# Two-layer hybrid decoder on one core: another order for VectorE's work in a pair of seven products

## The chip, the cores and the metric

The kernel runs on one core of one Trainium2 chip, as one program. The metric is the device time of an execution in microseconds (us), the median of three runs. The engines of the core are PE (TensorE), DVE (VectorE), ACT (ScalarE), POOL (GpSimd) and SP (SyncE, which here only issues DMAs); each runs its own list of instructions in order, and they hand over through semaphores.

## The reference

Two layers over T = 528 tokens (16 learned meta tokens ahead of 512), width 1024, in float32:

```
h = rms_norm(x, norm_g); z = h @ w_in                      # split into 11 parts
y_rnn = (rg_lru(x_rnn, ...) * silu(g_rnn)) @ rg_out
y_sc  = (sc_b * conv(sc_c * x_sc) * silu(g_sc)) @ sc_out
y_att = (mla(c_q, c_kv, k_rope, ...) * silu(g_att)) @ mla_out
gates = sigmoid(gate_logits + gate_b).reshape(b, t, 3, D)
merged = gates[:,:,0] * y_rnn + gates[:,:,1] * y_sc + gates[:,:,2] * y_att
return x + merged @ w_out
```

The change lies in the part that computes `gate_logits = h @ w_gates` for the three gates, and merges.

## The kernel before

**Numbers in two parts.** Every float32 operand of a matmul is held as a high part (rounded, `_hi`) and a low part (the rest, `_lo`), and a product is three matmuls: hi*hi, hi*lo, lo*hi. Weights come from HBM in units of 512 KB (128 partitions x 1024), into two staging buffers `w_raw`, and are split into a ring of four `w_hi` and `w_lo` buffers.

**The stages.** A layer runs NORM, CQ, ATT (four turns), RG (four turns), MR (four turns), MS (four turns), OUT. Only MR and MS are touched. There PE computes, in turn, a pair of gate tiles and one (MR) or two (MS) dense products `y`: MR turn i is pair a, y0, pair g, y1; MS turn i is pair g, y0, y1. The 12 pairs of a layer are PAIR_LIST; the first three (PLAIN) are plain products, the other nine, q = 0 to 8, are done by `seven`: the 2 x 2 block product in seven instead of eight block products (q = 0 to 4 in MR, q = 5 to 8 in MS).

**A pair of seven, engine by engine.** Its two units C and D give the four blocks of weights.
- DVE, `weight_sums(q)` (L1789): waits for both units and makes four sums S1 to S4 in `w_sum`, four instructions.
- ACT, `lead_upper(q, n)` (L1258): the high parts of blocks 0 to 3. Blocks 0 and 1 come from C, 2 from D, 3 is the first sum.
- POOL, `lead(q)` (L550): their low parts, two instructions each. Block 3 also waits for all four sums. Its first instruction raises `unit_split` by 2.
- ACT `sum_upper(q, n)` (L1264) and DVE `sum_lower(q, n)` (L1347): high and low parts of blocks 4 to 6, from the sums, when PE has left the ring's blocks.
- PE, `seven` (L883): products n = 0 to 6, 12 matmuls each. n = 0 waits for slot 0 to be free, n = 2 for slot 1; n = 0 to 3 for `lead_lo`, n = 4 to 6 for `sum_lo`; n = 5 also for gate sum 1, n = 6 for gate sum 2.
- ACT `keep_part` (L1276) and DVE `gate_sums` (L1804 to L1815): the first product is put aside and the block products are added up from PSUM in seven instructions: G1 (L1804) lets n = 5 write its bank, G2 (L1806) lets n = 6 write its own, then G3 (L1808); the last four (L1810, L1812, L1814, L1815) wait for n = 6, and L1814 and L1815 free the slots 0 and 1 for the next pair.
- ACT `open_gates(q)` (L1289): two tanh; the first waits for L1812, the second for both slots to be freed. Behind them DVE's `att_gate` or `merge` uses the gates.

**The order on ACT** (`open_pair`, unchanged): sum_upper(q, 0), keep_part(q), sum_upper(q, 1), sum_upper(q, 2), lead_upper(q+1, 0), lead_upper(q+1, 1), open_gates(q), lead_upper(q+1, 2), lead_upper(q+1, 3).

**The order on POOL**: lead(q), [branch_lower (L569) behind the a pairs], the split of the y unit or units (L471 one instruction, L476 four), lead(q+1).

**The loads on SP** (L383), in order of use: a unit is loaded when the unit two before it is split. So block 3 of lead(q) lets the unit Y of the next y product and unit C of pair q+1 go, and the split of Y lets unit D of pair q+1 go. In MS there are Y0 and Y1: lead(q) lets both go, Y0's split lets C go and Y1's split D.

Of the kernel before, what the change touches and what calls it, by code (L numbers as in the profile page):

```python
# [24 lines left out]
ALU = mybir.AluOpType  # L25
# [58 lines left out]
PLAIN = 3  # L84
# [81 lines left out]
def build(nc, xt, w_units, w_pair, params, hparams, consts, rope, stream):  # L166
    with ExitStack() as ctx:
# [5 lines left out]
        def sem(name):  # L173
            if name not in sems:
                sems[name] = ctx.enter_context(nc.semaphore(name))
            return sems[name]

        def at(name, l, i, k):

            stage, per = SIGNALS[name]  # L180
            first, this = (per, per) if isinstance(per, int) else (per[0], per[l])
            return sem(name), l * (STAGES[stage][0] * first) + i * this + (k + AHEAD.get(name, 0))
# [24 lines left out]
        def freed(stage, tile):  # L207

            return sem(f"slot_free{slot_of(stage, tile)}")
# [147 lines left out]
        def pair_used(l, p):  # L357

            if p < 0:
                return sem("unit_used"), unit_value("RG", l, 3, 5) + (RING + 1)  # L360
            stage, i, name, j = PAIR_LIST[p]
            return sem("unit_used"), unit_value(stage, l, i, j + 1) + (RING + 1)
# [982 lines left out]
        def _(dve):  # L1345
# [40 lines left out]
            for l in range(DEPTH):  # L1386
# [334 lines left out]
                def att_gate(i):  # L1721

                    for n in range(2):
                        dve.wait_ge(*was_read("RG", l, 3, "my1"))
                        dve.wait_ge(*gate_there(2 * i, n))
                        dve.scalar_tensor_tensor(kept(l, tile(xm, i * 2 + n)), kept(l, g_t[n][:]), 1.0,
                                                 kept(l, tile(xm, i * 2 + n)), ALU.add, ALU.mult).then_inc(
                                                     sem("att_gated"), 1)
# [62 lines left out]
                def sum_lower(q, n):  # L1791

                    dve.wait_ge(*at("sum_hi", l, q, n + 1))
                    lo_part(block_of(w_lo, 4 + n), raw_blocks(q)[4 + n], block_of(w_hi, 4 + n), "sum_lo")

                def gate_sums(q):

                    stage, i, name, j = PAIR_LIST[q + PLAIN]
                    w = SIDES[l]
                    bank = lambda s, a: ps[:, s, a, 0:w]  # L1800
                    first, second = (lambda n: g_t[n][:, side(l, 0)]), (lambda n: g_t[n][:, side(l, 1)])
                    dve.wait_ge(*at("block_used", l, q, 2))
                    dve.wait_ge(*at("part_kept", l, q, 1))
                    dve.tensor_tensor(first(0), bank(0, 1), second(0), ALU.add).then_inc(sem("gate_sum"), 1)  # L1804
                    dve.wait_ge(*at("block_used", l, q, 5))
                    dve.tensor_tensor(second(0), bank(0, 0), second(0), ALU.add).then_inc(sem("gate_sum"), 1)  # L1806
                    dve.wait_ge(*at("gate_sum", l, q, 2))
                    dve.tensor_tensor(second(1), bank(1, 0), second(0), ALU.add).then_inc(sem("gate_sum"), 1)  # L1808
                    dve.wait_ge(*pair_used(l, q + PLAIN))
                    dve.tensor_tensor(first(1), bank(0, 0), second(0), ALU.add).then_inc(sem("gate_sum"), 1)  # L1810
                    dve.wait_ge(*at("gate_sum", l, q, 4))
                    dve.tensor_tensor(second(0), bank(0, 1), second(1), ALU.add).then_inc(sem("gate_sum"), 1)  # L1812
                    dve.wait_ge(*at("gate_sum", l, q, 5))
                    dve.tensor_tensor(second(1), bank(0, 0), second(1), ALU.add).then_inc(freed(stage, f"{name}0"), 1)  # L1814
                    dve.tensor_tensor(first(1), bank(1, 1), first(1), ALU.add).then_inc(freed(stage, f"{name}1"), 1)  # L1815

# [84 lines left out]
                weight_sums(0)  # L1903
                mixes_lower(3)
                att_gate(1)
                for p in range(PLAIN, 8):
                    i = p // 2
                    if p % 2 == 0:
                        merge("MR", i - 1, 1)
                    for n in range(3):  # L1910
                        sum_lower(p - PLAIN, n)
                    gate_sums(p - PLAIN)
                    weight_sums(p - PLAIN + 1)
                    if p % 2 == 0:
                        att_gate(i)
                    else:
                        merge("MR", i, 0)
                merge("MR", 3, 1)
                for i in range(4):
                    q = 8 - PLAIN + i  # L1920
                    sum_lower(q, 0)
                    if i:
                        merged_lower(i - 1, 1)
                    sum_lower(q, 1)
                    sum_lower(q, 2)
                    gate_sums(q)
                    if i < 3:
                        weight_sums(q + 1)
                    merge("MS", i, 0)
                    merged_lower(i, 0)  # L1930
                    merge("MS", i, 1)
# [102 lines left out]
```

## Time and profile before

| what | value |
|---|---|
| median of 3 runs | 1707.01 us (1706.09 to 1707.89) |
| the profiled execution: time, span | 1710.13 us, 1708.3 us |
| busy in the span: PE, weight loads, POOL, DVE, ACT | 98%, 92%, 72%, 66%, 34% |
| mean granted TensorE clock | 0.997 |
| the chain that ended last, by engine | PE 74%, DVE 9%, POOL 6%, issue 6%, DMA 4%, ACT 1% |
| pairs of seven, layer 0 and layer 1 | 645.6 to 811.9 us and 1482.6 to 1648.9 us |

The span runs from the first to the last instruction; the 1.8 us around it belong to the run's time. Busy shares are averages over stages with different limits. "Idle before" is the time that an engine stood still ahead of an instruction, with what released it; "issue" means that the view names no releaser.

### The profile page before, as it was taken

How to read it: one execution, taken by the hardware profiler on the slowest of the kernel's cores; microseconds unless marked ns; L12 is line 12 of the kernel's file. 1: busy time of each engine (PE TensorE's matmuls, PEld its weight loads, DVE VectorE, ACT ScalarE, POOL GpSimd, SP SyncE). 2: the span in 40 equal slices, each digit the busy share in tenths (PEclk: the TensorE clock that was granted, in tenths of full speed). 3: DMA queues.
4: the chain of work that ended last, by engine and by line, in shares of the span. 5: the costliest groups of instructions: out<-in, count | busy, mean ns of one | idle time of the engine just before them, and what ended most of it. 6: DMA issues, size and time to landing. Idle time of an engine off the chain costs nothing.

```text
span 1708.3 us, 32114 instructions
## 1 busy us (share of the span) xinstructions
PE 1673.6 (98%) x11840; PEld 1569.9 (92%) x11840; DVE 1120.7 (66%) x1563; ACT 580.6 (34%) x1037; POOL 1228.4 (72%) x1345
## 2 busy tenths in 40 slices
PE   7999999999999999999999999999999999998999
PEld 7999999999999999999998888888889888887887
DVE  6966758485666687666349657574846667877651
ACT  4423333332343423323235232333323434243320
POOL 7764848385888687777867757484868996877684
PEclk9999999999999999999999999999999999999999
DMA  4432322132223232322532323132322223222333
GB/s 161 128 109 62 92 64 88 66 92 80 94 87 95 77 100 87 113 98 94 185 112 88 98 62 109 57 96 71 91 89 87 87 97 100 87 99 99 99 115 134
DMA packets 50008, 164.50 MB, mean 96 GB/s; under 512 B 6112, under 2 KB 7520, under 8 KB 49632
## 3 DMA queue, kind: packets, MB, share of 16 engines
q1 hardware_dynamic: 41904, 146.56, 27.0%
q10 hardware_dynamic: 8032, 17.00, 2.9%
q8 instruction: 44, 0.72, 0.2%
q14 instruction: 28, 0.23, 0.0%
HBM read 152.21 MB, written 10.81 MB: 95 GB/s over the span
## 4 chain that ended last, share of the span: by engine, by line
PE 74%; DVE 9%; POOL 6%; issue 6%; DMA 4%; ACT 1%; ACTq 0%; DVEq 0%; POOLq 0%; SPq 0%
PE slots L610 61%; DMA w_raw<-w_units 4%; PE slots L675 3%; POOL w_lo L476 3%; PE slots L709 3%; PE slots L883 2%; DVE weight_sums L1789 2%; PE slots L771 2%; POOL w_lo L550 2%; PE slots L693 1%; POOL w_hi L471 1%; DVE early L1515 1%; POOL branch_lo L569 1%; DVE early L1530 1%; PE slots L644 1%
## 5 line engine op out<-in xcount | busy, mean ns | idle before, releaser
L476 POOL TENSOR_TENSOR w_lo<-w_raw,w_hi 128x256 fp32r<-128x256 f32 x860 | 741.5, 892 | 17.9
L471 POOL TENSOR_SCALAR w_hi<-w_raw 128x1024 fp32r<-128x1024 f32 x215 | 259.0, 1205 | 245.2 <-PE slots L610 203.4
L610 PE MATMUL slots<-h_hi,w_hi 128*128 128x264 f32 (+1 forms) x1680 | 405.3, 308 | 0.7 <-DVE sc_pad L1643 0.7
L610 PE MATMUL slots<-h_lo,w_hi 128*128 128x264 f32 (+1 forms) x1680 | 399.9, 305 | 0.0
L610 PE MATMUL slots<-h_hi,w_lo 128*128 128x264 f32 (+1 forms) x1680 | 399.4, 304 | 0.0
L610 PEld LDWEIGHTS slots<-h_hi,w_hi 128*128 128x128 f32 x1680 | 271.0, 188 | 14.8 <-issue 1.6
L610 PEld LDWEIGHTS slots<-h_hi,w_lo 128*128 128x128 f32 x1680 | 270.0, 188 | 12.9
L610 PEld LDWEIGHTS slots<-h_lo,w_hi 128*128 128x128 f32 x1680 | 270.3, 188 | 12.0
L610 PE MATMUL slots<-branch_hi,w_hi 128*128 128x264 f32 (+1 forms) x552 | 143.9, 320 | 10.6 <-DVE branch_lo L1360 8.6
L610 PE MATMUL slots<-branch_lo,w_hi 128*128 128x264 f32 (+1 forms) x552 | 142.8, 318 | 0.0
L610 PE MATMUL slots<-branch_hi,w_lo 128*128 128x264 f32 (+1 forms) x552 | 142.4, 317 | 0.0
L550 POOL TENSOR_TENSOR w_lo<-w_raw,w_hi 128x256 fp32r<-128x256 f32 x108 | 89.8, 860 | 39.3 <-ACT w_hi L1258 39.3
L610 PEld LDWEIGHTS slots<-branch_hi,w_hi 128*128 128x128 f32 x552 | 92.2, 191 | 17.7 <-issue 11.1
L610 PEld LDWEIGHTS slots<-branch_hi,w_lo 128*128 128x128 f32 x552 | 91.9, 191 | 6.5
L610 PEld LDWEIGHTS slots<-branch_lo,w_hi 128*128 128x128 f32 x552 | 91.8, 191 | 6.2
L1105 ACT ACTIVATE residual_or_merged<-slots,r_bias,q_sc 128x144 f32<-128x144 f32 (+6 forms) x72 | 44.9, 623 | 149.2 <-DVE r_bias L1592 149.2
L883 PE MATMUL slots<-h_mixes_hi,w_hi 128*128 128x264 f32 (+1 forms) x288 | 82.8, 288 | 8.3 <-DVE w_lo L1347 7.3
L883 PE MATMUL slots<-h_mixes_lo,w_hi 128*128 128x264 f32 (+1 forms) x288 | 81.9, 284 | 0.0
L883 PE MATMUL slots<-h_mixes_hi,w_lo 128*128 128x264 f32 (+1 forms) x288 | 81.9, 284 | 0.0
L1258 ACT ACTIVATE w_hi<-w_raw 128x512 fp32r<-128x512 f32 x54 | 32.7, 628 | 112.7 <-DMA w_raw<-w_units 82.2
L883 PE MATMUL slots<-h_hi,w_hi 128*128 128x264 f32 (+1 forms) x216 | 62.0, 287 | 8.5 <-DVE gate_tanh L1804 8.2
L1347 DVE TENSOR_TENSOR w_lo<-weight_sums,w_hi 128x512 fp32r<-128x512 f32 x54 | 61.6, 1172 | 9.8 <-ACT w_hi L1264 9.8
(276 smaller groups left out, 3681.3 us busy)
## 6 DMA issues: line engine op xcount, KB each, us to landing
w_raw<-w_units SPq DMA_DIRECT2D x251, 512.0 KB, 3.6
stream<-sc_acc ACTq DMA_DIRECT2D x16, 264.0 KB, 2.1
x_old<-stream SPq DMA_DIRECT2D x16, 264.0 KB, 4.1
stream<-residual_or_merged ACTq DMA_DIRECT2D x16, 264.0 KB, 2.6
ab_raw<-w_units SPq DMA_DIRECT2D x8, 512.0 KB, 4.1
residual_or_merged<-xt ACTq DMA_DIRECT2D x4, 528.0 KB, 7.5
stream<-xt ACTq DMA_DIRECT2D x1, 2112.0 KB, 9.7
sc_back<-stream SPq DMA_DIRECT2D x2, 1056.0 KB, 5.8
```

The lines of the kernel that those rows point to most:

```text
L471: pool.tensor_scalar(hi, raw, 1.0, 1.0, ALU.mult, ALU.mult).then_inc(sem("hi_part"), 1)
L476: op = pool.tensor_tensor(lo[:, cols], raw[:, cols], hi[:, cols].bitcast(F32), ALU.subtract)
L550: op = pool.tensor_tensor(lo[:, cols], raw[:, cols], hi[:, cols].bitcast(F32), ALU.subtract)
L610: mm = pe.matmul(out[:, a_, 0:t1 - t0], w(k), x(k)[:, t0:t1], start=(n == 0), stop=(n == 3 * ks - 1))
L675: mm = pe.matmul(bank[:, 0:k1 - k0], q[:, q0:q0 + nq], k[:, k0:k1], start=(m == 0), stop=(m == 4 and not masked))
L709: mm = pe.matmul(out[:, a_, q0 - b0:q1 - b0], v[0:nk, j, h * VHEAD:(h + 1) * VHEAD], pt[0:nk, col + q0:col + q1], start=(j == 0 and n == 0 ...
L771: mm = pe.matmul(out[0:nt_, t % 4 // 2, (t % 2) * 256:(t % 2) * 256 + 256], x[:, k, t0:t0 + nt_], w[0][:, cols], start=(k == 0 and n == 0) ...
L883: mm = pe.matmul(out, block_of(ring, n)[:, k * P:(k + 1) * P], view(x, k), start=(m == 0), stop=(m == 11))
L1105: act.activation(dst, src, ACT.Exp, bias=r_bias[0:nq, n:n + 1], scale=q_sc[0:nq, c:c + 1], accum_out=r_sum[0:nq, n:n + 1]).then_inc(sem("p ...
L1258: act.activation(block_of(w_hi, n), raw_blocks(q)[n], ACT.Copy).then_inc(sem("lead_hi"), 1)
L1347: dve.tensor_tensor(dst, full, hi.bitcast(F32), ALU.subtract).then_inc(sem(signal), 1)
L1789: dve.tensor_tensor(out, x, y, ALU.add).then_inc(sem("w_summed"), 1)
```

## The change

DVE's list within a pair of seven is put in another order; no instruction is added or removed, and no other engine's list changes. Before, a pair is: three lower parts, all seven gate sums, the next pair's weight sums, then gates or merges. After, `gate_sums` comes in three parts and a new function `pair_sums` has the order: lower part 0, (in MS the lower part of the merged tile before), lower part 1, G1, lower part 2, G2 and G3, the next pair's four weight sums, the last four gate sums, then gates or merges.

```
--- before.py
+++ after.py
@@ -1793,26 +1793,29 @@
                     dve.wait_ge(*at("sum_hi", l, q, n + 1))
                     lo_part(block_of(w_lo, 4 + n), raw_blocks(q)[4 + n], block_of(w_hi, 4 + n), "sum_lo")
 
-                def gate_sums(q):
+                def gate_sums(q, part):
 
                     stage, i, name, j = PAIR_LIST[q + PLAIN]
                     w = SIDES[l]
                     bank = lambda s, a: ps[:, s, a, 0:w]
                     first, second = (lambda n: g_t[n][:, side(l, 0)]), (lambda n: g_t[n][:, side(l, 1)])
-                    dve.wait_ge(*at("block_used", l, q, 2))
-                    dve.wait_ge(*at("part_kept", l, q, 1))
-                    dve.tensor_tensor(first(0), bank(0, 1), second(0), ALU.add).then_inc(sem("gate_sum"), 1)
-                    dve.wait_ge(*at("block_used", l, q, 5))
-                    dve.tensor_tensor(second(0), bank(0, 0), second(0), ALU.add).then_inc(sem("gate_sum"), 1)
-                    dve.wait_ge(*at("gate_sum", l, q, 2))
-                    dve.tensor_tensor(second(1), bank(1, 0), second(0), ALU.add).then_inc(sem("gate_sum"), 1)
-                    dve.wait_ge(*pair_used(l, q + PLAIN))
-                    dve.tensor_tensor(first(1), bank(0, 0), second(0), ALU.add).then_inc(sem("gate_sum"), 1)
-                    dve.wait_ge(*at("gate_sum", l, q, 4))
-                    dve.tensor_tensor(second(0), bank(0, 1), second(1), ALU.add).then_inc(sem("gate_sum"), 1)
-                    dve.wait_ge(*at("gate_sum", l, q, 5))
-                    dve.tensor_tensor(second(1), bank(0, 0), second(1), ALU.add).then_inc(freed(stage, f"{name}0"), 1)
-                    dve.tensor_tensor(first(1), bank(1, 1), first(1), ALU.add).then_inc(freed(stage, f"{name}1"), 1)
+                    if part == 0:
+                        dve.wait_ge(*at("block_used", l, q, 2))
+                        dve.wait_ge(*at("part_kept", l, q, 1))
+                        dve.tensor_tensor(first(0), bank(0, 1), second(0), ALU.add).then_inc(sem("gate_sum"), 1)
+                    elif part == 1:
+                        dve.wait_ge(*at("block_used", l, q, 5))
+                        dve.tensor_tensor(second(0), bank(0, 0), second(0), ALU.add).then_inc(sem("gate_sum"), 1)
+                        dve.wait_ge(*at("gate_sum", l, q, 2))
+                        dve.tensor_tensor(second(1), bank(1, 0), second(0), ALU.add).then_inc(sem("gate_sum"), 1)
+                    else:
+                        dve.wait_ge(*pair_used(l, q + PLAIN))
+                        dve.tensor_tensor(first(1), bank(0, 0), second(0), ALU.add).then_inc(sem("gate_sum"), 1)
+                        dve.wait_ge(*at("gate_sum", l, q, 4))
+                        dve.tensor_tensor(second(0), bank(0, 1), second(1), ALU.add).then_inc(sem("gate_sum"), 1)
+                        dve.wait_ge(*at("gate_sum", l, q, 5))
+                        dve.tensor_tensor(second(1), bank(0, 0), second(1), ALU.add).then_inc(freed(stage, f"{name}0"), 1)
+                        dve.tensor_tensor(first(1), bank(1, 1), first(1), ALU.add).then_inc(freed(stage, f"{name}1"), 1)
 
 
 
@@ -1903,29 +1906,31 @@
                 weight_sums(0)
                 mixes_lower(3)
                 att_gate(1)
+                def pair_sums(q, between=None):
+
+                    sum_lower(q, 0)
+                    if between is not None:
+                        merged_lower(between, 1)
+                    sum_lower(q, 1)
+                    gate_sums(q, 0)
+                    sum_lower(q, 2)
+                    gate_sums(q, 1)
+                    if q + PLAIN + 1 < len(PAIR_LIST):
+                        weight_sums(q + 1)
+                    gate_sums(q, 2)
+
                 for p in range(PLAIN, 8):
                     i = p // 2
                     if p % 2 == 0:
                         merge("MR", i - 1, 1)
-                    for n in range(3):
-                        sum_lower(p - PLAIN, n)
-                    gate_sums(p - PLAIN)
-                    weight_sums(p - PLAIN + 1)
+                    pair_sums(p - PLAIN)
                     if p % 2 == 0:
                         att_gate(i)
                     else:
                         merge("MR", i, 0)
                 merge("MR", 3, 1)
                 for i in range(4):
-                    q = 8 - PLAIN + i
-                    sum_lower(q, 0)
-                    if i:
-                        merged_lower(i - 1, 1)
-                    sum_lower(q, 1)
-                    sum_lower(q, 2)
-                    gate_sums(q)
-                    if i < 3:
-                        weight_sums(q + 1)
+                    pair_sums(8 - PLAIN + i, i - 1 if i else None)
                     merge("MS", i, 0)
                     merged_lower(i, 0)
                     merge("MS", i, 1)
```

## Rows read from the trace of the kernel before

**Rows 1.** Who waited for whom: total us, times, longest us

```profile
PE slots L883 <- DVE gate_tanh L1804: 8.2, 6, 1.8
PE slots L883 <- DVE w_lo L1347: 7.3, 6, 1.8
...
DVE weight_sums L1789 <- issue: 39.5, 16, 5.6
```

**Rows 2.** Chain that ended last, in layer 1's pairs: start us, us, what

```profile
1509.17 3.58 POOL w_lo L476 x4
1512.76 3.26 DMA w_raw<-w_units
1518.88 1.24 DVE weight_sums L1789
```

**Rows 3.** Timeline of DVE, layer 0: start us, us, instruction, idle before

```profile
656.03 0.43 DVE L1810 TENSOR_TENSOR gate_tanh<-slots,gate_tanh 128x264 f32<-128x264 f32 x1 [2.00 <-PE slots L883]
...
657.31 0.42 DVE L1815 TENSOR_TENSOR gate_tanh<-slots,gate_tanh 128x264 f32<-128x264 f32 x1
660.06 0.69 DVE L1789 TENSOR_TENSOR weight_sums<-w_raw 128x512 f32<-128x512 f32 x1 [2.32 <-issue]
...
663.07 0.68 DVE L1789 TENSOR_TENSOR weight_sums<-w_raw 128x512 f32<-128x512 f32 x1
...
677.56 0.69 DVE L1789 TENSOR_TENSOR weight_sums<-w_raw 128x512 f32<-128x512 f32 x1 [0.19 <-issue]
...
794.71 0.69 DVE L1789 TENSOR_TENSOR weight_sums<-w_raw 128x512 f32<-128x512 f32 x1 [2.84 <-issue]
```

**Rows 4.** Timeline of ACT, layer 0, around the same pair

```profile
656.96 1.60 ACT L1289 ACTIVATE gate_tanh<-gate_tanh,channel_params 128x528 f32<-128x528 f32 x2 [0.98 <-DVE gate_tanh L1812]
660.00 0.63 ACT L1258 ACTIVATE w_hi<-w_raw 128x512 fp32r<-128x512 f32 x1 [1.43 <-DMA w_raw<-w_units]
```

**Rows 5.** Timeline of POOL, layer 0, around the same pair

```profile
653.54 2.81 POOL L476 TENSOR_TENSOR w_lo<-w_raw,w_hi 128x256 fp32r<-128x256 f32 x4
...
660.71 1.88 POOL L550 TENSOR_TENSOR w_lo<-w_raw,w_hi 128x256 fp32r<-128x256 f32 x2 [1.58 <-ACT w_hi L1258]
663.91 1.90 POOL L550 TENSOR_TENSOR w_lo<-weight_sums,w_hi 128x256 fp32r<-128x256 f32 x2 [1.32 <-DVE weight_sums L1789]
665.78 3.06 POOL L569 TENSOR_TENSOR branch_lo<-sc_back,branch_hi 128x528 fp32r<-128x528 f32 x2
668.81 1.49 POOL L471 TENSOR_SCALAR w_hi<-w_raw 128x1024 fp32r<-128x1024 f32 x1
670.38 3.56 POOL L476 TENSOR_TENSOR w_lo<-w_raw,w_hi 128x256 fp32r<-128x256 f32 x4
```

**Rows 6.** Timeline of SP's DMA issues, layer 0

```profile
673.98 0.33 SPq L383 DMA_DIRECT2D w_raw<-w_units  x1
```

**Rows 7.** Chain that ended last, in layer 0's pairs

```profile
739.43 6.33 PE slots L883 x36
...
757.53 10.24 PE slots L883 x84
767.77 11.72 PE slots L610 x96
```

**Rows 8.** Timeline of DVE, layer 1

```profile
1498.89 0.69 DVE L1789 TENSOR_TENSOR weight_sums<-w_raw 128x512 f32<-128x512 f32 x1 [3.15 <-issue]
...
1633.74 0.69 DVE L1789 TENSOR_TENSOR weight_sums<-w_raw 128x512 f32<-128x512 f32 x1 [4.33 <-issue]
```

**Rows 9.** Timeline of PE: one product 4, and product 2 of each layer's last pair

```profile
739.43 0.51 PE L883 MATMUL slots<-h_mixes_hi,w_hi 128*128 128x264 f32 x1 [1.84 <-DVE w_lo L1347]
...
804.59 0.28 PE L883 MATMUL slots<-h_mixes_hi,w_hi 128*128 128x264 f32 x1
...
1641.50 0.28 PE L883 MATMUL slots<-h_mixes_hi,w_hi 128*128 128x256 f32 x1
```

**Rows 10.** Stretch: PE, weight-load, DVE, ACT, POOL busy (count), PEclk, DMA share, GB/s

```profile
740.00:745.00 5.00, 5.00 (x30) 4.77 (x30) 3.09 (x5) 0.00 (x0) 4.83 (x7) 0.71 0.02 3
```

## The prediction

> **What bounds the kernel now.** I read the page first: PE is busy for 98% of the span, so in the stages without pairs there is nothing to gain, and the change touches none of them. Then the list of waits for PE in the pairs of seven: it stood still for 8.2 us in all ahead of product 5, waiting for G1 (L1804), and for 7.3 us ahead of product 4, waiting for lower part 0 [rows 1]. That is what the new order could win. The same list has the other side: ahead of the weight sums DVE waited 16 times, once in each pair that follows another, 39.5 us in all [rows 1]. "issue" names no releaser, but ACT's lead of block 2 starts at 660.00, released by the DMA of `w_raw` [rows 4], and the weight sums at 660.06 [rows 3]: both wait for unit D. The timelines of DVE, POOL, ACT and SP then give the order of events, and they show a loop beside PE's work. The chain that ended last runs through it in layer 1: split of Y (POOL), DMA of D, weight sums (DVE), and on to POOL again [rows 2].
>
> **The loop, measured.** Call T the start of the weight sums, which is D's landing. For the pair at T = 660.06:
> - the four sums end at 663.75, and POOL starts block 3 at 663.91, T + 3.85 [rows 3, 5];
> - block 3 takes 1.90, branch_lower follows to 668.81 and Y's split to 673.94, that is 1.49 + 3.56 less their overlap, so 10.0 after block 3 began [rows 5];
> - D's DMA is issued at 673.98 and the next weight sums start at 677.56, 3.6 later [rows 3, 6].
> Together 3.85 + 10.0 + 3.6 = 17.5, and 677.56 - 660.06 = 17.50. So this loop, not PE, dates each D. It has seven turns in a layer, from the pair q = 1 to q = 8: 660.06 to 794.71 is 134.65 us in layer 0 [rows 3], and 1498.89 to 1633.74 is 134.85 in layer 1 [rows 8]. PE's own pace is 10.24 for a seven and 11.72 for two y products [rows 7], so 16.1 in MR and 22.0 in MS: near the loop's pace, with no reserve in MR.
>
> **The change part by part.**
>
> *Lower part 2 behind G1, G2 behind it.* G1 moves up by one lower part, so product 5 no longer waits. G2 still ends when it did, since DVE has done the same work by then; PE would win some 1.1 of each 1.3 us. That is worth at most the 8.2 us [rows 1], and only while PE is what ends last.
>
> *The weight sums ahead of the last four gate sums.* Before, L1810 starts at 656.03 and the weight sums at 660.06, after 2.32 of waiting for D [rows 3]. Now DVE sits at the weight sums until 660.06 with the four gate sums behind them. They have the same instructions and durations, so the cost is who waits for them:
> - L1810 begins at T + 3.65. L1812 ends 0.9 later, which is the distance from 656.03 to ACT's tanh at 656.96 [rows 3, 4]; so ACT's tanh starts at T + 4.6. The two take 1.60 [rows 4], to T + 6.2.
> - Behind them in ACT's list stand the high parts of blocks 2 and 3. Before, block 2 went off at 660.00, when D landed [rows 4]; now it starts at T + 6.1 and takes 0.6.
> - POOL starts block 2 at T + 6.75, takes 1.88 and starts block 3 at T + 8.65 [rows 5], against T + 3.85.
> - L1815 ends 1.70 after L1810's start [rows 3], so slot 0 is free at T + 5.2.
>
> *What the loop does with it.* Block 3's first instruction lets Y and C be loaded. The loop gets 8.65 - 3.85 = 4.8 us longer, and nothing takes it up: the DMA of Y, its split and the DMA of D follow in series. Seven turns make 33.6 us a layer. The first turn's T does not move, for nothing ahead of it changes.
>
> *What shortens it again.* In the turns with branch_lower and in MS, Y's split runs beside DVE's lower parts: its four instructions took 3.56 there and 2.81 where DVE was quiet, and the L471 ahead of them was long as well [rows 5]. Together with L471 (1.49 against some 1.1) that is up to 1.2 a turn. In the new order the gates open from T + 5.4, the merges (663.7 to 667.6 before, four instructions of 3.9 in all) end at about T + 9.6 and the lower parts at T + 12. Y lands 0.95 (half of block 3) and 3.6 (a DMA) behind the start of block 3, at T + 13.2, so its split runs beside G1 to G3 only. Five of the seven turns can win this, 6.0 us; the other two are already quiet. Bounds: 27.6 and 33.6 us a layer. I take 28.6, near the quiet row, because DVE is mostly quiet then. The Trainium skill (GPSIMD Engine Reference, Specifications) says that GpSimd's way into SBUF is shared with VectorE and contended by Vector instructions with two SBUF inputs; the rows agree, and by it alone the sum would use 27.6.
>
> *What PE does with it.* In MR the y product now begins at about T + 17.6, when Y is split, and ends at T + 23.5; the next T is 8.65 + 10.0 + 3.6 - 1.0 = T + 21.3, and its slot 0 is free 5.2 later, at T + 26.5. So PE idles 3 us ahead of product 0, 0.7 ahead of product 2 and 1 ahead of Y. In MS a turn of 25 to 26 stands against 22.0. What counts is the last pair of each layer. Its product 2 began at 804.59, T + 9.9, in layer 0 [rows 3, 9] and at 1641.50, T + 7.8, in layer 1 [rows 8, 9]; now it begins at T + 8.75, when block 2 is there, and product 3 another 0.45 late, as block 3 takes 1.9 and a product 1.46 (10.24 / 7 [rows 7]). That is -0.7 in layer 0 and +1.4 in layer 1, less 0.3 of a wait for G1 there that goes. Nothing moves in the tail behind it.
>
> *The sum.* 2 x 28.6 - 0.7 + 1.1 = 57.6 us on the profiled execution's 1710.13 us (span 1708.3 and 1.8 around it). That execution lay 3.1 above the median; on the median it makes 1764.6, and I say 1765. The 8.2 us of waits for G1 are not taken off: PE waits for weights then.
>
> *The clock.* Ahead of one product 4 PE stood still for 1.84 us [rows 9]; in the stretch behind it the granted clock was 0.71, part of it at 1.2 instead of 2.4 GHz [rows 10], and 36 matmuls took 6.33 us [rows 7] where 36/84 of 10.24 is 4.39. The new idle times are as long or longer. One such loss of 1.9 a pair lies in the 3 us of waiting for the slot and costs nothing; in the last pair it shows. Bounds 0 and 4 us for both layers; I take 0 and keep 4 in the range.
>
> **The rivals.**
>
> *Faster: D is there in time.* If D landed before product 6 is near its end, the weight sums would fill the 2.00 us in which DVE waits for PE ahead of L1810 [rows 3], and PE would keep some 7 of the 8.2 us: 1700. It decides where D lands when DVE falls idle, at 654.0 instead of 660.06, some 6 us sooner: then the last gate sums come 3.7 - 2.0 = 1.7 late, and the slots are needed only one y product later. All 16 waits of [rows 1] speak against it: D came last in every pair.
>
> *No change: the loads don't hang on the sums.* If Y and C had been let go early by something else, T would stay, and PE would lose only what shows in the last pairs: -0.7 + 1.1 = 0.4, so 1707.4. The exact sum of 17.50 from the rows speaks against it.
>
> *Much slower: the clock stays down.* If the idle times put whole pairs at 1.2 GHz, a pair of MR would need 32 us of PE, from T + 5.2 to T + 37.4, against the T + 26.5 at which the next may begin: 10.9 more in each of four MR pairs, 44 us a layer, 1853 in all, more with MS. For it: the stretch of [rows 10]. Against it: the same rows, where it passed within the pair. The Trainium skill (TensorE: Matmul & The Clock Gate, section HAM oscillation) says that waits for data between groups of matmuls can put each group back at half rate; for short spells that is the 0 to 4 us above, for whole pairs this rival.
>
> **How the numbers follow.** The lengthened loop has 0.88: it needs only the lists' order and D's landing. D in time 0.05, no change 0.03, the low clock 0.04. The forecast's own range is 2 x 27.6 + 0.4 = 55.6, so 1762.6, to 2 x 33.6 + 0.4 + 4 = 71.6, so 1778.6. I widen it to 1752 to 1781: 10 us below for a loop that gains more from a quiet DVE than those rows show (0.75 us a turn), 2 above for other contention. Within 0.2%, or 3.4 us, a measurement of this kernel can't tell two kernels apart; faster 0.05, same 0.03, slower 0.92.
>
> **What the profile after would show.** Right: block 3 (L550) of each pair starts 8.65 us behind the weight sums; the weight sums from q = 1 to q = 8 lie some 163 us apart instead of 134.65; ACT's block 2 comes behind both tanh; PE waits ahead of product 0 for L1814 (2 to 3 us in MR), ahead of product 2 for L550; the waits for L1804 are gone; PE's busy time is as before or, with the clock, a little longer. Wrong: weight sums that start without a wait; a distance from block 3 to the next T that shrinks by more than 1.2 us; PE busy for much longer at a low granted clock.

## The result and the profile after

The changed kernel took 1748.30 us (median of 4 runs, 1745.45 to 1750.73) against 1707.01 (4 runs, 1706.09 to 1707.89). The ratio is 1.0241, with an interval of 1.0224 to 1.0259: slower by 41 us. The prediction was 1765 us, in a range from 1752 to 1781: its sign came true, and so did the chain of waits that it named; its size was some 17 us too large, which puts the measured time below the range. The profiled execution took 1748.56 us, with a span of 1746.8, which is 38.5 more than before; this is what the account below is held against.

The page of the changed kernel: busy time and share of each engine, and the chain that ended last by engine.

```profile
PE 1685.0 (96%) x11840; PEld 1571.5 (90%) x11840; DVE 1089.2 (62%) x1563; ACT 575.8 (33%) x1037; POOL 1210.2 (69%) x1345
...
PE 68%; DVE 11%; POOL 9%; DMA 6%; issue 4%; ACT 2%; ACTq 0%; DVEq 0%; SPq 0%; POOLq 0%
```

PE has fallen from 74% of the chain to 68%. DVE and POOL stand for more of the chain than before, although both were busy for less of the time (DVE had 66% of the shorter span, POOL 72%). A chain that leaves the busiest engine for engines that are less busy points to a loop of dependencies; the chain itself is shown below.

The waits of the changed kernel: who waited for whom, total us, times, longest us.

```profile
DVE weight_sums L1789 <- DMA w_raw<-w_units: 136.0, 18, 11.5
ACT gate_tanh L1289 <- DVE gate_tanh L1815: 135.0, 18, 10.1
POOL w_lo L550 <- ACT w_hi L1258: 119.7, 24, 8.1
...
PE slots L883 <- DVE gate_tanh L1817: 21.9, 13, 3.0
PE slots L610 <- POOL w_lo L476: 12.8, 13, 1.4
...
PE slots L883 <- POOL w_lo L550: 6.0, 15, 0.7
```

The waits for G1 and for lower part 0 of [rows 1] are gone, as the new order could promise. In their place the first three lines show three engines standing in a row behind one DMA: DVE waits for unit D (136.0 us against 39.5 before), ACT's tanh waits for the gate sums behind DVE's weight sums, and POOL waits for ACT. PE's new waits are for the slot (L1817 frees slot 0), for the split of Y (L476) and for the lower parts of the leads (L550).

The pair that [rows 3 to 5] show before, now after. DVE:

```profile
658.95 0.69 DVE L1789 TENSOR_TENSOR weight_sums<-w_raw 128x512 f32<-128x512 f32 x1 [5.82 <-DMA w_raw<-w_units]
659.68 1.42 DVE L1789 TENSOR_TENSOR weight_sums<-weight_sums,w_raw 128x512 f32<-128x512 f32 x2
661.01 0.69 DVE L1789 TENSOR_TENSOR weight_sums<-w_raw 128x512 f32<-128x512 f32 x1
661.62 0.43 DVE L1813 TENSOR_TENSOR gate_tanh<-slots,gate_tanh 128x264 f32<-128x264 f32 x1
...
679.43 0.69 DVE L1789 TENSOR_TENSOR weight_sums<-w_raw 128x512 f32<-128x512 f32 x1 [6.77 <-DMA w_raw<-w_units]
...
813.64 0.69 DVE L1789 TENSOR_TENSOR weight_sums<-w_raw 128x512 f32<-128x512 f32 x1 [10.46 <-DMA w_raw<-w_units]
```

ACT:

```profile
662.54 1.61 ACT L1289 ACTIVATE gate_tanh<-gate_tanh,channel_params 128x528 f32<-128x528 f32 x2 [7.53 <-DVE gate_tanh L1815]
664.05 0.61 ACT L1258 ACTIVATE w_hi<-w_raw 128x512 fp32r<-128x512 f32 x1
```

POOL:

```profile
664.75 1.44 POOL L550 TENSOR_TENSOR w_lo<-w_raw,w_hi 128x256 fp32r<-128x256 f32 x2 [6.60 <-ACT w_hi L1258]
666.14 2.35 POOL L550 TENSOR_TENSOR w_lo<-weight_sums,w_hi 128x256 fp32r<-128x256 f32 x2
668.45 3.51 POOL L569 TENSOR_TENSOR branch_lo<-sc_back,branch_hi 128x528 fp32r<-128x528 f32 x2
671.92 1.05 POOL L471 TENSOR_SCALAR w_hi<-w_raw 128x1024 fp32r<-128x1024 f32 x1
673.06 2.80 POOL L476 TENSOR_TENSOR w_lo<-w_raw,w_hi 128x256 fp32r<-128x256 f32 x4
```

Read against T = 658.95: L1813 starts at T + 2.67, the tanh at T + 3.6, ACT's block 2 at T + 5.1, POOL's block 2 at T + 5.8 and its block 3 at T + 7.2. The prediction had T + 3.65, 4.6, 6.1, 6.75 and 8.65. So every step is there, in the order forecast, and early by 1.0 from the very first. (Of the fourteen turns in both layers, twelve have block 3 at T + 7.1 to 7.3, and two, q = 1 and q = 5 of layer 1, at T + 7.7.) The reason stands in DVE's rows: the four weight sums took 2.75 us, where they took 3.7 before (660.06 to 663.75 in [rows 3]). POOL's row gives the other 0.4: its two instructions of block 2 took 1.44 and not 1.88.

The chain that ended last, in the same pair: start us, us, what.

```profile
655.39 3.48 DMA w_raw<-w_units
...
658.95 0.70 DVE weight_sums L1789
...
664.05 1.14 ACT w_hi L1258 x2
...
668.49 2.57 POOL branch_lo L569 x2
...
671.92 1.06 POOL w_hi L471
...
673.06 2.81 POOL w_lo L476 x4
675.89 3.46 DMA w_raw<-w_units
```

It is the loop of the prediction, round once, without a single piece of PE. One turn is now 679.43 - 658.95 = 20.48 us, where it was 17.50.

**The account of the 38.5 us.** T is the start of a pair's weight sums, and it moved as follows.

| | layer 0 | layer 1 | forecast, each |
|---|---|---|---|
| first T of the loop (q = 1) to the last (q = 8), before | 134.65 | 134.85 | |
| the same, after (658.95 to 813.64; 1516.80 to 1670.90) | 154.69 | 154.10 | |
| difference | +20.0 | +19.3 | +28.6 |
| of it, T to block 3, seven turns | +23.4 | +24.2 | +33.6 |
| of it, block 3 to the next T, seven turns | -3.4 | -4.9 | -5.0 |
| last T to the y product behind the last pair (811.90 and 830.12; 1648.94 and 1687.28) | -0.7 | +1.2 | -0.7, +1.1 |

Together 20.0 + 19.3 - 0.7 + 1.2 = 39.8; the first T came 1.1 sooner in layer 0, and 0.3 sooner in layer 1 by its distance from that y product of layer 0; 39.8 - 1.4 = 38.4. The line of T to block 3 is off by some 10 us a layer, and it is the one that holds the duration of the weight sums. The last line agrees by luck, as shown further down.

### The profile page after: what moved, and what is told of

Its sections match the earlier page's. It is cut to its first block, busy times and chain, and to the rows that moved or that the text cites. A ratio compares the mean times of both kernels' runs of the same rounds, so it can differ in the third digit from the quotient of the medians.

```text
span 1746.8 us, 32114 instructions
## 1 busy us (share of the span) xinstructions
PE 1685.0 (96%) x11840; PEld 1571.5 (90%) x11840; DVE 1089.2 (62%) x1563; ACT 575.8 (33%) x1037; POOL 1210.2 (69%) x1345
## 4 chain that ended last, share of the span: by engine, by line
PE 68%; DVE 11%; POOL 9%; DMA 6%; issue 4%; ACT 2%; ACTq 0%; DVEq 0%; SPq 0%; POOLq 0%
PE slots L610 58%; DMA w_raw<-w_units 6%; POOL w_lo L476 4%; POOL w_lo L550 3%; PE slots L675 3%; DVE weight_sums L1789 2%; PE slots L709 2%; PE slots L771 2%; POOL w_hi L471 2%; PE slots L693 1%; ACT w_hi L1258 1%; DVE early L1515 1%; POOL branch_lo L569 1%; DVE early L1530 1%; PE slots L644 1%
## 5 line engine op out<-in xcount | busy, mean ns | idle before, releaser
L476 POOL TENSOR_TENSOR w_lo<-w_raw,w_hi 128x256 fp32r<-128x256 f32 x860 | 730.0, 879 | 17.9
L550 POOL TENSOR_TENSOR w_lo<-w_raw,w_hi 128x256 fp32r<-128x256 f32 x108 | 83.2, 799 | 119.7 <-ACT w_hi L1258 119.7
L1789 DVE TENSOR_TENSOR weight_sums<-w_raw 128x512 f32<-128x512 f32 x36 | 26.3, 731 | 136.0 <-DMA w_raw<-w_units 136.0
L883 PE MATMUL slots<-h_hi,w_hi 128*128 128x264 f32 (+1 forms) x216 | 63.7, 295 | 21.9 <-DVE gate_tanh L1817 21.9
L1289 ACT ACTIVATE gate_tanh<-gate_tanh,channel_params 128x528 f32<-128x528 f32 (+1 forms) x36 | 26.3, 730 | 137.3 <-DVE gate_tanh L1815 135.0
```

The lines of the kernel that those rows point to most:

```text
L476: op = pool.tensor_tensor(lo[:, cols], raw[:, cols], hi[:, cols].bitcast(F32), ALU.subtract)
L550: op = pool.tensor_tensor(lo[:, cols], raw[:, cols], hi[:, cols].bitcast(F32), ALU.subtract)
L883: mm = pe.matmul(out, block_of(ring, n)[:, k * P:(k + 1) * P], view(x, k), start=(m == 0), stop=(m == 11))
L1289: act.activation(kept(l, g_t[n][:]), kept(l, g_t[n][:]), ACT.Tanh, bias=param(l, which, i * 2 + n), scale=(0.5, -0.5)[n]).then_inc(sem("ga ...
L1789: dve.tensor_tensor(out, x, y, ALU.add).then_inc(sem("w_summed"), 1)
```

## The experiments

Each ratio is to the kernel before, run in turn with it on the same chip; its medians there were 1709.12 us (e1 to e4), 1710.56 (e5 to e8) and 1707.59 (e9, e10), so compare ratios rather than times. "Block 3" is the start of POOL's third block behind T, in the pair q = 1 of layer 0.

### Is it ACT's leads behind the gates? (e1_leads_first)

The changed kernel, with one other order on ACT: the high parts of the next pair's blocks 2 and 3 go ahead of the tanh again, so that they no longer wait for the gate sums. The slot is then still late for PE.

```
# open_pair, on ACT
                     if more:
                         lead_upper(q + 1, 0)
                         lead_upper(q + 1, 1)
-                    open_gates(q)
-                    if more:
                         lead_upper(q + 1, 2)
                         lead_upper(q + 1, 3)
+                    open_gates(q)
```

> The changed kernel, but ACT makes the high parts of blocks 2 and 3 of the next pair ahead of both tanh. DVE's order stays, so the slots are still freed behind the weight sums. Loop theory (the change costs because block 3, and with it the next loads, comes late): block 3 starts on POOL about 3.9 us behind the weight sums again, the weight sums of q = 1 to q = 8 lie 133 to 137 us apart, and the time is 1706 to 1712 us. Slot theory (the change costs because PE waits for the slots, 21.9 us in the changed kernel): those waits stay, and the time is 1725 us or more.

Measured: 1713.21 us, ratio 1.0021 (1.001 to 1.0032). The weight sums start at 657.07 and block 3 at 660.92, at T + 3.85, exactly the distance of before. From q = 1 to q = 8 it takes 134.90 and 137.19 us. The waits of PE in it:

```profile
PE slots L883 <- DVE gate_tanh L1813: 16.0, 11, 3.2
...
PE slots L610 <- POOL w_lo L476: 1.9, 2, 1.4
```

PE still stands for 16.0 us ahead of product 0 for the freed slot, and the kernel has lost 0.2% and not 2.4%. So nearly all of the loss went by way of ACT's block 2 and POOL's block 3; the theory that the slot is what costs, falls. Two numbers lie just above what was expected: the time (1713.21 against at most 1712) and layer 1's 137.19 us (at most 137). In MS the turns from q = 6 to q = 8 took 22.2 us in both layers, where they were 21.3 to 21.6 before, so the late slot may not be quite free; its price is at most the 0.2%.

### Why 1.45 us a turn less than forecast? (e2_block2_first)

The changed kernel, with ACT's block 2 ahead of the tanh and only block 3 behind them. POOL's block 2 then runs beside the weight sums again, as before the change, but block 3 stays late.

```
# open_pair, on ACT
                         lead_upper(q + 1, 1)
+                        lead_upper(q + 1, 2)
                     open_gates(q)
                     if more:
-                        lead_upper(q + 1, 2)
                         lead_upper(q + 1, 3)
```

> The changed kernel, but ACT makes the high part of block 2 alone ahead of both tanh; block 3 stays behind them. If POOL and DVE slow each other down (contention theory), the four weight sums take 3.7 us again instead of 2.7, because POOL works on block 2 beside them; block 3 starts 6.8 us behind the weight sums instead of 7.2, and the time falls by only 6 us, to 1742. If they don't, the sums stay at 2.7 us, block 3 starts at 5.8, and the time falls by 20 us, to 1728.

Measured: 1745.21 us, ratio 1.021 (1.0193 to 1.0228). DVE's timeline in it:

```profile
660.61 0.69 DVE L1789 TENSOR_TENSOR weight_sums<-w_raw 128x512 f32<-128x512 f32 x1 [6.05 <-DMA w_raw<-w_units]
661.34 2.36 DVE L1789 TENSOR_TENSOR weight_sums<-weight_sums,w_raw 128x512 f32<-128x512 f32 x2
663.62 0.68 DVE L1789 TENSOR_TENSOR weight_sums<-w_raw 128x512 f32<-128x512 f32 x1
```

and POOL's:

```profile
661.26 1.89 POOL L550 TENSOR_TENSOR w_lo<-w_raw,w_hi 128x256 fp32r<-128x256 f32 x2 [1.55 <-ACT w_hi L1258]
...
667.40 0.74 POOL L550 TENSOR_TENSOR w_lo<-weight_sums,w_hi 128x256 fp32r<-128x256 f32 x1 [4.25 <-ACT w_hi L1258]
```

With POOL beside them (661.26 to 663.15) the two middle sums take 2.36 us; without, in the changed kernel, 1.42. The sums are back at 3.7 in all, and block 3 starts at T + 6.8. The time was expected at 1742 us and came out 3 above it, since only part of the 0.4 us a turn arrived: the seven turns lie 153.10 and 152.54 us apart, 1.6 less in each layer than in the changed kernel. The two orders come out within 0.3% of each other, for opposite reasons: here block 2 is off the path and the sums are slow, there block 2 is on it and the sums are fast. This shows 0.95 of the missing 1.45: the changed kernel made its own path shorter, because it took POOL away from beside the sums. The other 0.44 is block 2 itself, 1.89 us in this kernel's row and 1.44 in the changed kernel's.

One form of the weight sums, over all pairs, in three kernels (least, median and longest ns). The changed kernel:

```profile
L1789 DVE TENSOR_TENSOR weight_sums<-weight_sums,w_raw x36: 691/692/1118, 639.1 to 1672.4; 128x512 f32<-128x512 f32 x36
```

The kernel before:

```profile
L1789 DVE TENSOR_TENSOR weight_sums<-weight_sums,w_raw x36: 691/1115/1219, 640.0 to 1635.7; 128x512 f32<-128x512 f32 x36
```

This experiment:

```profile
L1789 DVE TENSOR_TENSOR weight_sums<-weight_sums,w_raw x36: 691/1115/1217, 640.6 to 1672.8; 128x512 f32<-128x512 f32 x36
```

### The two halves of the change (e3_g1_only, e4_sums_only)

One keeps G1 ahead of lower part 2, but has the weight sums behind all gate sums, as before:

```
# pair_sums, on DVE
                     gate_sums(q, 1)
+                    gate_sums(q, 2)
                     if q + PLAIN + 1 < len(PAIR_LIST):
                         weight_sums(q + 1)
-                    gate_sums(q, 2)
```

> Only the first part of the change: G1 ahead of lower part 2 (and in MS the merged tile's lower part ahead of lower part 1, as before); the weight sums stay behind all gate sums. Loop theory: the waits for G1 (8.2 us) go, but the loop of loads dates the next pair, so the time falls by 0 to 3 us, 1704 to 1707. If PE's waits simply add up, it falls by 7 us, to 1700.

Measured: 1705.47 us, ratio 0.9982 (0.9971 to 0.9992). The waits of PE in it:

```profile
PE slots L883 <- DVE w_lo L1347: 9.2, 7, 1.9
...
PE slots L883 <- DVE gate_tanh L1805: 2.0, 5, 1.2
```

The wait for G1 is down from 8.2 us [rows 1] to 2.0, and the gain is some 3 us: the loop, which this half doesn't touch, dates the pairs (134.15 and 135.36 us from q = 1 to q = 8), so that PE mostly waits elsewhere instead.

The other moves the weight sums ahead of the last gate sums and leaves G1 behind the three lower parts:

```
# pair_sums, on DVE
                     sum_lower(q, 1)
-                    gate_sums(q, 0)
                     sum_lower(q, 2)
+                    gate_sums(q, 0)
                     gate_sums(q, 1)
```

> Only the second part of the change: the weight sums ahead of the last four gate sums, with G1 behind all three lower parts as before. Loop theory: as the whole change, 1745 to 1751 us, since PE waits for weights anyway. If G1's place is worth its 8.2 us of waits, 1755 us or more.

Measured: 1748.66 us, ratio 1.0239 (1.0221 to 1.0256), with 154.42 and 155.32 us from q = 1 to q = 8. This half is the whole loss, and beside it the other half gains nothing that can be measured.

### The other order of the kernel before (e5_pool_waits)

The kernel before, in which POOL waits for the four sums ahead of block 2 instead of block 3. The sums then run alone; block 2 comes behind them.

```
# lead, on POOL
-                        if n == 3:
+                        if n == 2:
                             pool.wait_ge(*at("w_summed", l, q, 4))
```

> The kernel before, with one wait moved: POOL waits for all four weight sums ahead of block 2 instead of ahead of block 3. If POOL and DVE slow each other down, the sums now take 2.7 us instead of 3.7, block 2 takes about 1.4 us, block 3 starts 4.2 to 4.7 us behind the weight sums instead of 3.85, and the time is 1709 to 1717 us. If they don't, block 3 starts at 5.7 us and fourteen turns of the loop make it 1733 us.

Measured: 1714.18 us, ratio 1.0018 (1.0007 to 1.0028). DVE's timeline in it:

```profile
660.29 0.69 DVE L1789 TENSOR_TENSOR weight_sums<-w_raw 128x512 f32<-128x512 f32 x1 [2.15 <-issue]
661.02 1.42 DVE L1789 TENSOR_TENSOR weight_sums<-weight_sums,w_raw 128x512 f32<-128x512 f32 x2
662.36 0.69 DVE L1789 TENSOR_TENSOR weight_sums<-w_raw 128x512 f32<-128x512 f32 x1
```

and POOL's:

```profile
663.19 1.90 POOL L550 TENSOR_TENSOR w_lo<-w_raw,w_hi 128x256 fp32r<-128x256 f32 x2 [3.66 <-DVE weight_sums L1789]
665.05 1.90 POOL L550 TENSOR_TENSOR w_lo<-weight_sums,w_hi 128x256 fp32r<-128x256 f32 x2
```

The sums take 2.75 us in the old order too, once POOL stands still. That settles it: it is POOL's company and not the place in DVE's list that sets their duration. Block 3 starts at T + 4.76, above the 4.2 to 4.7 expected, because block 2 took 1.90 here and 1.44 in the changed kernel. It ran beside the merges in both, and met them at another place; what that does is told in the last section. Had the sums kept their 3.7 us, block 3 would have come at about T + 5.7. About half of that longer wait was paid back by the quicker sums. The time lost still less, because the way from block 3 to the next T got shorter too, 105.0 us over the seven turns of layer 0 against 107.6 before; no run takes that apart.

### Is the loop what paces the kernel? (e6 to e8, e10)

If it is, letting Y go sooner helps the kernel before as well. Y's staging buffer held the unit C; all of its readers are done with block 2 (POOL) and the fourth sum (DVE), so the load needn't wait until block 3 has begun. The edit, with `q` given only for the first y unit behind a pair of seven:

```
# load, on SP
-                sp.wait_ge(sem("unit_split"), unit_value(stage, l, i, j) + 1)
+                if q is None:
+                    sp.wait_ge(sem("unit_split"), unit_value(stage, l, i, j) + 1)
+                else:
+                    sp.wait_ge(*at("lead_lo", l, q, 2))
+                    sp.wait_ge(*at("w_summed", l, q, 4))
```

On the kernel before:

> The kernel before, but SP lets unit Y of a y product (Y0 in MS) go when the low parts of blocks 0 and 1 and the four weight sums are made, instead of with block 3's first half (MS's loads on SP are written out instead of looped, for waits on constants). Loop theory: each turn gets about 1 us shorter, down to PE's own pace (16.1 in MR, 22.0 in MS), so MR's turns are 15.9 to 16.6 us instead of 16.7 and 17.5, PE's waits shrink, and the time is 1697 to 1704 us. If PE alone sets the pace before, nothing moves: 1706 to 1709 us.

Measured: 1700.53 us, ratio 0.9936 (0.9916 to 0.9956). From q = 0 to q = 8 the T's lie 150.73 and 150.48 us apart, where they were 155.46 and 155.51, so 9.8 us of the 10.1 by which the span is shorter are the loop's. The prediction's loop is confirmed by a change in the other direction. Half of the expectation was wrong. Almost half of the 9.8 us came from the first turn of each layer, q = 0 to q = 1 (20.80 and 20.66 us before, 18.72 and 18.06 now), which it didn't mention. In layer 0's MR the two later turns without branch_lower fell, from 16.69 and 18.18 us to 15.91 and 17.08. The two with it stayed, 17.51 and 17.57 before, 17.64 and 17.76 now: by the order of the lists, because branch_lower stands ahead of Y's split on POOL, and an earlier Y just waits.

The MS loads had to be written out for that edit, so one kernel has only this, on the kernel before:

```
# the loads, on SP
-                with sp.Fori(0, 4) as i:
+                for i in range(4):
                     for j in range(4):
                         load("MS", l, i, j)
```

> A control for the early load: the kernel before with nothing but MS's loads on SP written out instead of looped. The turn into MS took 18.18 us in layer 0, 1.5 us more than its like; if that is the entry of the loop, it falls to 16.7 us, and the time by at most 1 us, since PE has reserve in MS: ratio 0.999 to 1.000. If the early load's gain came from here, it is 0.995 or less.

Measured: 1708.31 us, ratio 1.0004 (0.9992 to 1.0017). The gain of the early load isn't from there, and layer 0's turn into MS stays at 17.84 us (18.18 before), above the 16.68 of the other turn of MR that has no branch_lower. In layer 1 it took 16.26 us before and 16.12 here, so the entry of the loop on SP isn't the reason; what is, stays open.

The early load together with the half of the change that helps (G1 ahead of lower part 2):

> The same early load of Y with G1 ahead of lower part 2 (the weight sums behind all gate sums). With the loop out of the way the waits for G1 are worth their full size: 1692 to 1699 us, 4 to 7 us below the early load alone. If the loop still dates each pair, it is within 2 us of the early load alone.

Measured: 1698.15 us, ratio 0.9928 (0.9908 to 0.9948), 149.54 and 149.50 us from q = 0 to q = 8. Expected was a further gain of 4 to 7 us, measured were 2, and the two intervals separate that neither from nothing nor from 4. The waits for G1 went from 9.9 us to 1.6, and the time didn't follow by as much. DVE still waited ahead of the weight sums in every pair, for 0.26 to 6.73 us, so the loop still dates them.

The early load on the whole change:

> The whole change with the early load of Y. Loop theory: Y lands 6.4 us behind the weight sums instead of 11.8; where POOL has no branch_lower to do first (the even turns of MR and those of MS), its split starts about 2.7 us sooner, four or five turns a layer, so 1720 to 1730 us. If the loads don't matter and PE's waits for slots and blocks are the cost, it stays at 1745 us or more.

Measured: 1731.28 us, ratio 1.0109 (1.0093 to 1.0126); the loops of the two layers are 165.65 and 166.61 us, 9.6 and 7.3 less than in the changed kernel. That is 1 us above the range expected. About half of the change's loss comes back through one wait on SP, with DVE's order as it is (1.1% is left of 2.4%; of the span's 38.5 us, 16.8 come back). It comes back where it was expected: in layer 0's MR the turns without branch_lower fell from 19.69 and 20.59 us to 17.35 and 17.61, those with it stayed (20.48 and 21.49 against 20.40 and 21.64). By the order of POOL's list, blocks 2 and 3 and branch_lower stand ahead of Y's split, and in the changed order they are late themselves.

### A version that beats both (e9_branch_late)

e6 named the next piece of the loop. On top of the early load and G1's new place, POOL's branch_lower goes behind the split of the next Y:

```
# on POOL
                 for i in range(4):
                     split_unit("MR", l, i, 2, 2)
+                    if i:
+                        branch_lower(i - 1)
                     split_pair(2 * i + 1)
                     split_unit("MR", l, i, 5, 3)
                     split_pair(2 * i + 2)
-                    branch_lower(i)
                 for i in range(4):
                     for j in (2, 3):
                         split_unit("MS", l, i, j)
+                        if i == 0 and j == 2:
+                            branch_lower(3)
```

> The early load of Y and G1 ahead of lower part 2, and POOL does branch_lower behind the split of the next Y instead of ahead of it. In the kernel with the early load the turns with branch_lower stayed at 17.1 to 17.7 us, while the others fell to 16.0. Loop theory: these turns fall to 16.1 to 16.6 us too, and the time by 2 to 5 us, to 1693 to 1696 us (ratio 0.990 to 0.992). If branch_lower's place is of no account, the time stays within 1 us of 1698 us (0.993).

Measured: 1690.70 us against 1707.59, ratio 0.9899 (0.9878 to 0.992). Its page:

```profile
PE 1666.3 (99%) x11840; PEld 1564.6 (93%) x11840; DVE 1106.0 (66%) x1563; ACT 580.2 (34%) x1037; POOL 1229.7 (73%) x1345
```

The expectation gave 1693 to 1696 us and a ratio from 0.990; the time is 2 us below that range and the ratio at its edge. (It also said that the turns with branch_lower had stayed at 17.1 to 17.7 us; 17.08 was the turn into MS, which has none.) From one block 3 to the next it takes 15.6 to 17.0 us in layer 0's MR, near PE's own 16.1 (from 10.24 and half of 11.72, [rows 7]), and DVE no longer waited for D ahead of layer 0's first three pairs. PE is busy for 99% of the span, which is 1687.3 us, 21.0 less than before. Of these, 12.8 us lie between the T's of q = 0 and q = 8 (150.56 and 147.61 us against 155.46 and 155.51); layer 0's first T came 5.3 us sooner too, which this account doesn't explain.

## Why the prediction was wrong

**Right: what bounds the kernel.** The loop beside PE, and not PE at 98%, dated the pairs. The seven turns a layer grew by 39.3 us in all, with a span that grew by 38.5; e1 gave it back by shortening the loop alone, with PE's 16.0 us of waits for the slot left in; e6 and e9 gained by shortening it below what it was before the change.

**Right: who is late.** "The cost is who waits for them": tanh, ACT's block 2, POOL's block 2, block 3, in this order. e4 shows that the moved weight sums do all of it, e1 that they do it through ACT's list.

**The step that failed: "They have the same instructions and durations".** The term is T to block 3: 8.65 us forecast, 7.2 measured, so the loop grew by 3.35 us a turn and not by 4.8. It was mis-sized in two places, both taken from rows of [rows 3, 5] in which DVE and POOL worked at the same time. The four sums took 3.7 us there, because POOL's block 2 ran beside them. In the new order block 2 waits for the tanh, which wait for the gate sums, which wait for the weight sums: POOL must stand still while they run, and they took 2.75 (1.0 a turn). POOL's block 2 took 1.88 beside the sums and 1.44 beside DVE's later work (0.44 a turn). Fourteen turns of 1.45 are 20.3 of the 57.6 us; 37.3 is what the sum would then have been, against 38.5. Moving the weight sums was the very thing that changed their company, and the prediction asked only whether Y's split would be quieter. e2 and e5 show both directions.

**Right in size, in part by luck: what shortens it again.** 5.0 us a layer were taken, 3.4 and 4.9 came. The turn shown above has three parts: Y's split is quiet (1.05 and 2.80 us against 1.49 and 3.56 in [rows 5], 1.2 less), but block 3 took 2.35 instead of 1.90 and branch_lower 3.51 instead of 3.06, both beside DVE's merge and lower parts. So this turn won 0.4 us of the 1.2. The prediction had only the first part. Its total came near because other turns made up for it: the two that it had called quiet already won 0.4 and 1.0 us in layer 0, and one with branch_lower (q = 3) lost 0.6.

**Right in number, by luck: the last pairs.** -0.7 and +1.2 us, forecast -0.7 and +1.1. Product 2 of the last pair began at T + 7.5 in both layers, not at T + 8.75, for the reason above, and by that alone PE could have begun the y product behind the pair at T + 15.3 and T + 15.1, against 17.2 and 15.2 before. In its place PE stood still for POOL's split of Y0, which the prediction had put at nothing for these pairs:

```profile
830.12 0.51 PE L610 MATMUL slots<-branch_hi,w_hi 128*128 128x264 f32 x2 [1.22 <-POOL w_lo L476]
...
1687.28 0.50 PE L610 MATMUL slots<-branch_hi,w_hi 128*128 128x512 f32 x1 [1.33 <-POOL w_lo L476]
```

Two errors of some 1.25 us each cancelled.

**Right: the slot costs little.** Forecast was a slot free at T + 5.2 and 3 us of idle PE ahead of product 0 in MR. It is free sooner, for product 0 starts at 663.03, at T + 4.1 (again the quicker sums); the longest wait was 3.0 and the 13 made 21.9. That such waits cost little, at most 0.2%, e1 shows.

**Right: the clock.** Taken at 0. In the pairs it was low in one place, around the longest wait for the slot. PE's timeline of the changed kernel, and the stretch from there (as in [rows 10]):

```profile
745.37 0.58 PE L883 MATMUL slots<-h_hi,w_hi 128*128 128x264 f32 x1 [3.02 <-DVE gate_tanh L1817]
```

```profile
745.40:750.80 5.40, 5.40 (x24) 5.40 (x25) 4.47 (x6) 2.83 (x6) 3.80 (x5) 0.50 0.04 5
```

The granted clock was 0.50, that is 1.2 GHz, and 24 matmuls took 5.44 us, where 2.93 is what they take at 2.4 GHz (24/84 of 10.24 [rows 7]). The 2.5 us didn't reach the next T: those weight sums still waited 9.31 us for the DMA of D, at 765.76. What the Trainium skill says (TensorE: Matmul & The Clock Gate, HAM oscillation), that waits for data between groups of matmuls can put each group back at half rate, was seen in the first products of this one pair, and not in one pair after another. Over the profiled execution the mean granted clock was 0.997, as before.

**The rivals.** "D is there in time" is refuted by the 18 waits of DVE for the DMA, 136.0 us in all. "No change" is refuted by the T's. "The clock stays down" is refuted by that mean of 0.997. No rival was the cause; the case called likeliest was, with a smaller price. Its own lower bound of 1762.6 had no room for a shorter T to block 3, and the 10 us below it were meant for another part of the loop.

## What to carry to other kernels

A busy PE may still be paced by a loop that runs beside it: add up one turn from the rows of every queue in it, and if the sum is the distance between two turns, cost a change by what it does to that sum and not by the waits on PE. Take the duration of a moved instruction from a row in which the same engines run beside it as will in the new order; if none is there, keep the quiet and the shared duration as the two bounds. And when a load's release hangs on a late reader, look who the last true reader is: here this gained more than the new order of DVE.

## What the runs showed of the hardware

**DVE and POOL slow each other, depending on where the operands are.** The sum of two 128x512 tiles in SBUF took 0.69 us on DVE alone and 1.1 to 1.2 us beside POOL; POOL's lower part of 128x256 took 0.72 alone and about 0.95 in the same time (half of 1.44 and of 1.88, the two instructions of block 2). The GPSIMD Engine Reference of the Trainium skill (Specifications) says that GpSimd shares its SBUF interfaces with VectorE, and that DVE instructions with two SBUF inputs contend for them. The runs agree, and give the size. They also show the other side: gate products with one operand in PSUM and one in SBUF hardly moved over 32 instructions, also where POOL's lower parts ran at the same time (one at 664.75). The changed kernel, the product and the sum behind it (least, median and longest ns):

```profile
L1735 DVE SCALAR_TENSOR_TENSOR gated<-gate_tanh,slots x32: 674/690/707, 619.6 to 1698.7; 128x528 f32<-128x528 f32 x16, 128x512 f32<-128x512 f32 x16
...
L1739 DVE TENSOR_TENSOR residual_or_merged<-residual_or_merged,gated x32: 691/1000/1714, 620.4 to 1699.4; 128x528 f32<-128x528 f32 x16, 128x512 f32<-128x512 f32 x16
```

The same instructions kept DVE busy for 1120.7 us before and 1089.2 after, and POOL for 1228.4 and 1210.2: the slower kernel had less busy time on both, because they ran beside each other less.

**The one that starts later pays.** In the kernel before, 37 of the 72 weight sums started while an instruction of POOL was running, and took 0.79 to 1.23 us. The other 35 took 0.68 to 0.69, also the 17 during which POOL started one. So it isn't enough to know that two instructions overlap. In the changed kernel POOL's block 2 (664.75) was under way when DVE's merge sum started (665.48), and it was the sum that took 1.27 us; in e5 the merge sum started first and block 2 took the longer time.

**The clock was low after waits of different length.** Its granted value was 0.71 behind a wait of 1.84 us before the change [rows 9, 10] and 0.50 behind one of 3.02 us after it; behind one of 2.48 us, ahead of product 0 at 724.70 in the changed kernel, it stood at 1.00 in the stretch of 5.3 us that followed. The length of a wait alone doesn't say what it does to the clock, and no run here separates what does.
